# First-branch scores by halves of the rows, and queries split a tile at a time

## What is computed

```python
h = rmsnorm(x, g_mix); z = h @ w_in            # queries, keys, values of both branches, two gates
qa, ka, va, qb, kb, vb, ga, gb = split(z)
# branch A: 8 query heads over 2 key/value heads of 64, per-head rmsnorm, 2-D rotary
q = axial(rmsnorm(qa, q_gain)); k = axial(rmsnorm(ka, k_gain))
s = einsum("bqkgd,bskd->bkgqs", q, k) * scale; o = softmax(s) @ v
# branch B: dilated windows, 3 groups of 4 heads, combined by softmax denominators
x = x + (sigmoid(ga) * (o @ w_a_out) + sigmoid(gb) * (b @ w_b_out)) @ w_out
x = x + square(relu(rmsnorm(x, g_mlp) @ w_up)) @ w_down
```

## Time and profile before

| | us |
|---|---|
| median of 3 runs (1193.88 to 1195.73) | 1195.72 |
| the profiled execution | 1193.6 |
| its span | 1191.8 |
| TensorE busy | 1153.5 (97%) |
| DVE, ACT, POOL busy | 561.5, 414.8, 320.7 |
| share of TensorE in the chain that ended last | 87% |
| first key unit begins / last key unit ends | 40.4 / 87.0 |
| a key unit (81.4 to 87.0) | 5.6 |
| wait for the broadcast of the norms, once, before 56.9 | 3.5 |
| first and last scores of branch A begin | 92.7 / 248.2 |
| waits ahead of scores of branch A at 92.7, 99.9 and 112.0 | 2.0, 1.4, 0.2 |
| product with the values, a prompt unit of A (103.5 to 104.3) | 0.8 |
| granted TensorE clock, mean | 0.994 |

### The profile page before, as it was taken

One profiled execution on the slowest core, in us unless ns is written; L12 is line 12 of the kernel. 1 busy time (PEld: TensorE's weight loads), 2 busy tenths in 40 slices (PEclk: granted clock), 3 DMA queues, 4 the chain that ended last, 5 costly groups with the idle time before them and its releaser, 6 DMA issues.

```text
span 1191.8 us, 16489 instructions
## 1 busy us (share of the span) xinstructions
PE 1153.5 (97%) x6186; PEld 1040.9 (87%) x6186; DVE 561.5 (47%) x1007; ACT 414.8 (35%) x929; POOL 320.7 (27%) x244
## 2 busy tenths in 40 slices
PE   8898999989999999999999999999999999999997
PEld 6776898977889999999788989898898989898896
DVE  7576654555554342422615635344352625344354
ACT  7436666655455321221324312213130212212122
POOL 6311102020111150441713232415041332415120
PEclk9999999999999999999999999999999999999999
DMA  9301020200202030221522012222221112222202
GB/s 349 100 11 61 1 72 1 71 1 3 70 1 72 12 101 19 71 89 57 191 71 69 11 63 71 72 70 70 70 70 37 47 57 70 70 70 70 70 0 106
DMA packets 47125, 77.15 MB, mean 65 GB/s; under 512 B 7648, under 2 KB 18272, under 8 KB 47072
## 3 DMA queue, kind: packets, MB, share of 16 engines
q1 hardware_dynamic: 43488, 71.83, 18.2%
q10 hardware_dynamic: 3584, 4.61, 1.1%
HBM read 73.20 MB, written 3.22 MB: 64 GB/s over the span
## 4 chain that ended last, share of the span: by engine, by line
PE 87%; DVE 7%; issue 3%; ACT 2%; DMA 0%; ACTq 0%; DVEq 0%
PE unit_ps L691 18%; PE unit_ps L692 17%; PE unit_ps L693 17%; PE score_ps L691 7%; PE score_ps L692 7%; PE score_ps L693 7%; PE out_ps L824 4%; PE turn_ps L805 2%; DVE q_lo L1495 1%; PE score_ps L795 1%; PE unit_ps L752 1%; PE score_ps L752 1%; PE out_ps L752 1%; PE score_ps L770 1%; PE turn_ps L919 1%
## 5 line engine op out<-in xcount | busy, mean ns | idle before, releaser
L666 POOL TENSOR_TENSOR ring_lo<-ring_whole,ring_hi 128x512 fp32r<-128x512 f32 x236 | 311.9, 1343 | 832.9 <-ACT ring_hi L951 832.6
L691 PE MATMUL score_ps<-act_hi,ring_hi 128*128 128x384 f32 x512 | 171.3, 335 | 0.0
L693 PE MATMUL score_ps<-act_hi,ring_lo 128*128 128x384 f32 x512 | 171.1, 334 | 0.0
L692 PE MATMUL score_ps<-act_lo,ring_hi 128*128 128x384 f32 x512 | 171.1, 334 | 0.0
L961 ACT ACTIVATE relu<-score_ps 128x384 f32<-128x384 f32 x64 | 31.5, 493 | 380.2 <-PE score_ps L693 380.2
L951 ACT ACTIVATE ring_hi<-ring_whole 128x512 fp32r<-128x512 f32 x236 | 143.5, 625 | 42.0 <-DMA ring_whole<-in_w_up 22.5
L693 PE MATMUL unit_ps<-ring_hi,u_lo 128*128 128x512 f32 x384 | 151.3, 394 | 0.0
L691 PE MATMUL unit_ps<-ring_hi,u_hi 128*128 128x512 f32 x384 | 151.3, 394 | 0.0
L692 PE MATMUL unit_ps<-ring_lo,u_hi 128*128 128x512 f32 x384 | 151.3, 394 | 0.0
L1332 DVE TENSOR_TENSOR x<-x,unit_ps 128x512 f32<-128x512 f32 x96 | 65.8, 686 | 177.2 <-PE unit_ps L693 177.2
L691 PE MATMUL unit_ps<-ring_hi,act_hi 128*128 128x512 f32 x336 | 144.4, 430 | 1.3 <-DVE mix_part L1471 1.2
(11 more groups left out here) (174 smaller groups left out, 1797.2 us busy)
## 6 DMA issues: line engine op xcount, KB each, us to landing
ring_whole<-in_w_up SPq DMA_DIRECT2D x64, 256.0 KB, 4.6
ring_whole<-in_w_down SPq DMA_DIRECT2D x64, 256.0 KB, 4.4
ring_whole<-in_w_in SPq DMA_DIRECT2D x47, 256.0 KB, 4.7
ring_whole<-in_w_in SPq DMA_DIRECT2D x64, 128.0 KB, 2.9
ring_whole<-in_w_out SPq DMA_DIRECT2D x16, 256.0 KB, 4.1
xT<-in_x_turned SPq DMA_DIRECT2D x16, 192.0 KB, 4.7
x_in<-in_x_prompt SPq DMA_DIRECT2D x4, 512.0 KB, 6.8
ring_whole<-in_w_a_out SPq DMA_DIRECT2D x8, 256.0 KB, 4.7
```

Source lines behind the costliest of these rows:

```text
L666: pool.tensor_tensor(ring_lo[:, slot, :], ring_whole[:, slot, :], ring_hi[:, slot, :].bitcast(F32), ALU.subtract).then_inc(lo_cut, 1)
L691: pe.matmul(out, sta[0], mov[0], start=first, stop=False)
L692: pe.matmul(out, sta[0], mov[1], start=False, stop=False)
L693: return pe.matmul(out, sta[1], mov[0], start=False, stop=last)
```

## The change

Scores of branch A are issued for two units at a time, as branch B's are: one of each key head, the one on rows 0 to 63 and the other on rows 64 to 127, three products over 64 rows each. The pair waits for the exponential of the unit before it. The units are ordered so that heads g and g + 4 are neighbours. Queries are rotated by DVE straight from the banks to `q_tok` (the second ACT copy goes; DVE's cosine product frees the bank); the step `turn_q` transposes a whole query tile when its first attention unit is added to the list, and splits it into `q_hi` and `q_lo`, each once, for four heads on both halves of the rows. Keys have one high and one low tile. `scale_q` stands behind the last `take_qa`. At most one tile waits for its transpose in the key units, and there are three token buffers for five.

```diff
-TOK_BUFS = 5
+TOK_BUFS = 3
...
-        branch_a += [("A", t, [(h, 0, 4)]) for h in range(A_HEADS)]
+        branch_a += [("A", t, [(x * A_GROUP + g, 0, 4)]) for g in range(A_GROUP) for x in range(A_KV)]
...
-        branch_a += [("A", t, [(h, 4, 2), (h + 1, 4, 2)]) for h in range(0, A_HEADS, 2)]
+        branch_a += [("A", t, [(h, 4, 2), (h + 1, 4, 2)]) for h in (0, A_GROUP, 2, A_GROUP + 2)]
...
             units.append(new)
-            steps.append(("q_split", len(units) - 1))
+            if new[2][0][0] == 0:
+                steps.append(("turn_q", new[1]))
...
-            paired = i < len(units) and units[i][0] != "A" and i % 2 == 0
-            if paired and units[i - 1][0] != "A":
+            paired = i < len(units) and i % 2 == 0
+            early = paired and i and units[i - 1][0] != "A"
+            if early:
...
     def take_qa(t):
         steps.append(("take_qa", t))
-        waiting.append(("qa", t))
...
             take_qa(t + 2)
-        while len(waiting) > 3:
+            if t + 2 == TILES - 1:
+                steps.append(("scale_q",))
+        while len(waiting) > 1:
             turn_next()
...
-        q_hi = sb(ctx, "q_hi", [P, 2, 2, P], F32R)
-        q_lo = sb(ctx, "q_lo", [P, 2, 2, P], F32R)
+        q_hi = sb(ctx, "q_hi", [P, 2, A_GROUP, P], F32R)
+        q_lo = sb(ctx, "q_lo", [P, 2, A_GROUP, P], F32R)
...
             def scores_a(u):
+
                 _, t, segs = units[u]
-                bank = score_ps[u % 2]
                 if u == 0:
                     pe.wait_ge(qa_free, TILES)
-                pe.wait_ge(queries_split, u + 1)
...
+                else:
+                    pe.wait_ge(expd, u)
+                pe.wait_ge(*free_of(turn_free, plan.turn_no[("turn_q", t)]))
+                for tt in {seg[1] + seg[2] - 1 for seg in segs}:
+                    pe.wait_ge(*free_of(turn_free, plan.turn_no[("turn_qk", "kva", tt)]))
+                for j in range(len(segs)):
+                    for product in range(3):
+                        for x in range(2):
+                            h, k0, nk = units[u + x][2][j]
+                            rows = slice(x * HD, (x + 1) * HD)
+                            q = (q_lo if product == 2 else q_hi)[rows, t % 2, h % A_GROUP, :]
+                            k = (k_lo if product == 1 else k_hi)[rows, k0 * P:(k0 + nk) * P]
+                            last = pe.matmul(score_ps[x][:, j * nk * P:(j + 1) * nk * P], q, k, start=(product == 0),
+                                             stop=(product == 2))
...
+                elif kind == "turn_q":
+                    n, t = plan.turn_no[s], s[1]
+                    pe.wait_ge(q_ready, t + 1)
+                    wait_bank(pe, turn_free, n)
+                    for c in range(A_GROUP):
+                        last = pe.transpose(turn_ps[n % 2][:, c * P:(c + 1) * P], q_tok[:, t, c * P:(c + 1) * P],
+                                            ident[:, :])
+                    last.then_inc(turned, 1)
...
-                act.activation(qk_sq[:, :], bank[:, :], ACT.Square)
-
-                act.activation(buf.rearrange("p (g k d) -> p g k d", g=A_GROUP, k=A_KV),
-                               bank[:, :].rearrange("p (k g d) -> p g k d", k=A_KV, g=A_GROUP),
-                               ACT.Copy).then_inc(qa_free, 1)
+
+                act.wait_ge(qk_squares, plan.square_no[("take_qa", t)])
+                act.activation(qk_sq[:, :], qa_banks[t][:, :], ACT.Square).then_inc(qa_squared, 1)
...
+                elif kind == "scale_q":
+                    act.wait_ge(q_sums, 1)
+                    act.activation(q_scale[:, :], q_scale[:, :], ACT.Sqrt).then_inc(q_roots, 1)
...
+                elif kind == "turn_q":
+                    n, t = plan.turn_no[s], s[1]
+                    act.wait_ge(turned, n + 1)
+                    if t >= 2:
+
+                        act.wait_ge(scored, last_of_tile[t - 2] + 1)
+                    act.activation(q_hi[:, t % 2, :, :], turn_ps[n % 2][:, :].rearrange("p (h t) -> p h t", h=A_GROUP),
+                                   ACT.Copy).then_inc(turn_hi, 1)
...
+            def rotate_q(t):
+
+                bank, buf = qa_banks[t], q_tok[:, t, :]
...
+                dve.wait_ge(qa_squared, t + 1)
+                dve.tensor_reduce(q_scale[:, t * A_HEADS:(t + 1) * A_HEADS],
+                                  qk_sq[:, :].rearrange("p (h d) -> p h d", d=HD), AX_X, ALU.add).then_inc(qk_squares, 1)
...
+                for x in range(2):
+                    dve.tensor_tensor(turned_pairs[:, :, :, x, :], pairs[:, :, :, 1 - x, :],
+                                      sines[:, :, x, :].unsqueeze(1).broadcast_to([P, A_HEADS, 2, 16]), ALU.mult)
...
+                dve.tensor_tensor(buf, bank[:, :].rearrange("p (k g d) -> p k g d", **heads),
+                                  rope_qc[:, pos, :].unsqueeze(1).unsqueeze(1).broadcast_to([P, A_KV, A_GROUP, HD]),
+                                  ALU.mult).then_inc(qa_free, 1)
+                dve.wait_ge(qa_free, t + 1)
+                dve.tensor_tensor(buf, buf, rot_q[:, :].rearrange("p (k g d) -> p k g d", **heads),
+                                  ALU.add).then_inc(q_ready, 1)
...
-                dve.wait_ge(scored, u + 1 if branch == "A" else (u // 2 + 1) * 2)
+                dve.wait_ge(scored, (u // 2 + 1) * 2)
...
+                elif kind == "turn_q":
+                    n, t = plan.turn_no[s], s[1]
+                    dve.wait_ge(turn_hi, plan.split_no[s] + 1)
+                    lo_of_turn(q_hi[:, t % 2, :, :], q_lo[:, t % 2, :, :],
+                               turn_ps[n % 2][:, :].rearrange("p (h t) -> p h t", h=A_GROUP))\
+                        .then_inc(turn_free[n % 2], 1)
```

More of the change, by code:

```diff
@@ L191, in attend @@
                 steps.append(("turn_p", i - 2))
-            if paired and units[i - 1][0] == "A":
+            if paired and not early:
                 steps.append(("scores_pair", i))
@@ L518, in build @@
         keys_hi = sem("keys_hi")
[L519 to L520 removed]
+        qa_squared = sem("qa_squared")
+        q_ready = sem("q_ready")
         scored = sem("scored")
@@ L572, in block_end @@
             return plan.unit_no[("unit", name, 7 if name[0] in "gy" else TILES - 1)] + 1
[L574 to L579, removed]
+        last_of_tile = {units[u][1]: u for u in range(len(units)) if units[u][0] == "A"}
         def class_order(branch, t):
@@ L758, in scores_a @@
                 _, t, segs = units[u]
-                bank = score_ps[u % 2]
                 if u == 0:
                     pe.wait_ge(qa_free, TILES)
-                pe.wait_ge(queries_split, u + 1)
[L763 to L772, removed]
+                else:
[12 more added lines that the diff above has]
+                                             stop=(product == 2))
+                            if product == 2 and j == len(segs) - 1:
+                                last.then_inc(scored, 1)
             def scores_pair(u):
@@ L892, in _ @@
                     last.then_inc(turned, 1)
-                elif kind == "scores" and units[s[1]][0] == "A":
-                    scores_a(s[1])
                 elif kind == "scores_pair":
-                    scores_pair(s[1])
+                    (scores_a if units[s[1]][0] == "A" else scores_pair)(s[1])
                 elif kind == "turn_p":
@@ L1079, in _ @@
                         dst = qkT_c[:, class_buffer(name[2], t), :]
[L1080 to L1081 removed]
                     elif name == "kva":
[L1083 to L1087 removed]
+                        act.activation(k_hi[:, t * P:(t + 1) * P], turn_ps[n % 2][:, 0:P], ACT.Copy).then_inc(keys_hi, 1)
                         continue
@@ L1096, in _ @@
                     take_unit(s[1], s[2])
-                elif kind == "q_split":
-                    u = s[1]
-                    _, t, segs = units[u]
-                    act.wait_ge(*free_of(turn_free, plan.turn_no[("turn_qk", "qa", t)]))
-                    if u >= 2:
-                        act.wait_ge(scored, u - 1)
-                    for out in range(2):
-                        last = act.activation(q_hi[out * HD:(out + 1) * HD, u % 2, 0:len(segs), :], queries(u)[0],
-                                              ACT.Copy)
-                    last.then_inc(queries_hi, 1)
+                elif kind == "turn_q":
[5 more added lines that the diff above has]
+                                   ACT.Copy).then_inc(turn_hi, 1)
                 elif kind == "scores":
@@ L1419, in _ @@
                 elif kind == "take_qa":
-                    rotate_a("qa", s[1])
+                    rotate_q(s[1])
+                elif kind == "scale_q":
+                    scale_queries()
                 elif kind == "norm2":
@@ L1484, in _ @@
                     dve.wait_ge(keys_hi, t + 1)
-                    for kv in range(A_KV):
-                        rows, other = slice(kv * HD, (kv + 1) * HD), slice((1 - kv) * HD, (2 - kv) * HD)
```

(13 more changed lines are left out.)

70 lines of the change are left out of this document (33 added, 37 removed).

## The result

The changed kernel takes 1197.03 us (median of 20 runs, 1196.14 to 1198.35), the kernel before, measured beside it, 1195.46 (20 runs, 1191.55 to 1196.85). The ratio is 1.0017, with an interval of [1.001, 1.0023]: slower, by 1.2 to 2.7 us. The direction was forecast, the size (+10) was not.

A forecast was written before the change was run, and what follows sets the result against it. TensorE, busy in 97% of the span, was taken as the bound. The terms 1.6 - 2.2 + 8.0 + 1.5 + 1.1 + 0 gave +10.0 us on 1193.6, so 1203.6 us; 8-in-10 range 1190 to 1213.

The forecast's parts named there:

- The end: Last two pairs, held by the transposes of the third group's last unit, which do not move: 0 us.
- The other ticks: Remaining branch A ticks: 4.2 us of low-half waits go, 5.3 us of new waits for exponentials come: +1.1 us.
- the early start: First pairs issued inside the last key unit: pair 0 waits 3.8 us, pair 2 5.1, plus clock dips; net +8.0 us.
- PE work of the scores: TensorE's work on branch A's 20 pairs: the saved product in four is eaten by mode switches, 0 us.
- Start of the key units: First key unit starts later because DVE, not ACT's copy, now frees the query bank: +1.6 us.
- Key units 2 to 4: Key tile low-half wait and its clock dip go, -4.0 us; key tile 3's transpose waits 1.8: net -2.2 us.
- Tick 7: Transposes of query tile 1 and key tile 5 take both turn banks; the next wait 3.0 us: +1.5 us.
- the rival in which the halves don't overlap: Branch A pairs: products on the two row halves run in series, giving 1217.6 us; chance 0.08.
- The relief: Rival: DVE is far enough ahead that no new wait replaces the old ones, giving 1181.8 us; chance 0.22.
- the even exchange: Rival: new waits only match those replaced, with the early start at 3.4 us, giving 1195.6 us; chance 0.18.

The follow-up runs named there:

- the cuts moved: POOL's cuts of weight chunks moved off the unit's end in four unit groups: changed kernel 1189.76 us (ratio 0.9957), kernel before 1187.83 us (0.9943).
- the late start: The changed kernel with branch A's first tick three ticks later, where the kernel before had it: 1194.77 us, ratio 1.0006 to the kernel before.
- early maxima: The changed kernel with both maxima of a branch A pair taken at once and unit 1's exponential ahead of the last key unit's root: 1188.58 us, ratio 0.9954.
- free banks: The changed kernel with query tiles 0 and 1 in two transpose banks, so the first key unit needs no wait for DVE: 1194.65 us, ratio 1.0001.
- pair behind the values: The changed kernel with a pair of branch A issued behind its tick's product with the values instead of ahead: 1194.41 us, ratio 1.0001.

## Why the prediction was wrong

The step that failed is "The end: 0": the last two pairs do stand where they stood, 14.9 us behind the first unit of the gates in both kernels (381.61 and 385.21), but the pairs of branch B ahead of them cost 4.0 us less than before. "The other ticks: +1.1" failed next, by 2.9. The waits of the early start, the largest term, were right in kind and near in size.

| step | forecast | found in the rows |
|---|---|---|
| PE work of the scores | 0 | +0.3 |
| Start of the key units | +1.6 | +1.5 |
| Key units 2 to 4 | -2.2 | -3.1 |
| The early start | +8.0 | +6.9 |
| Tick 7 | +1.5 | +2.8 |
| The other ticks | +1.1 | -1.8 |
| The end | 0 | -4.0 |
| sum | +10.0 | +2.6 |

**PE work: right in sum, and by luck.** An odd tick and the even one behind it, with the first product of the unit that follows each, in the changed kernel:

```profile
169.62 0.60 PE L813 MATMUL turn_ps<-ident,probs 128*128 128x128 f32 x4
170.06 1.06 PE L832 MATMUL out_ps<-v_a,probsT 128*128 128x128 f32 x8
170.87 0.60 PE L694 MATMUL unit_ps<-ring_hi,act_hi 128*128 128x512 f32 x1
...
172.48 0.60 PE L813 MATMUL turn_ps<-ident,probs 128*128 128x128 f32 x4
173.01 0.50 PE L777 MATMUL score_ps<-k_hi,q_hi 64*128 64x512 f32 x2
...
173.91 1.16 PE L832 MATMUL out_ps<-v_a,probsT 128*128 128x128 f32 x8
174.82 0.60 PE L694 MATMUL unit_ps<-ring_hi,act_hi 128*128 128x512 f32 x1
```

The pair takes 0.90 us (0.85 forecast) and 0.53 pass ahead of it; the transposes of an odd tick take 0.44. Without the values that is 1.87 us, as forecast, and the rival in which the halves don't overlap is out. But the values behind a pair, which the prediction left out, take 0.91 us (173.91 to 174.82) against 0.81 in the odd tick. With them two ticks take 2.34 + 1.25 = 3.59 us, and before 2 x 1.71 = 3.42 (102.55 to 104.26): 0.17 more a pair, some 3.4 us over the 20 pairs. What hides it was not forecast either. In the kernel before, transposes ahead of a score that is held up took longer than the 0.36 counted:

```profile
170.63 0.60 PE L805 MATMUL turn_ps<-ident,probs 128*128 128x128 f32 x4
171.37 0.50 PE L770 MATMUL score_ps<-kT_a,q_hi 128*128 128x512 f32 x1
```

At nine ticks these transposes took 0.60 to 0.74 us beside any listed wait, some 2.6 us more than counted in all, and nearly all of that is gone. In sum: from the first key unit to the gates' first unit are 326.3 us before (40.41 to 366.68) and 327.4 after (42.89 to 370.28); without the waits inside (21.5 and 20.6) and the dips (5.1 and 6.8) 299.7 and 300.0 are left, +0.3.

**Start, key units, early start, tick 7: right in kind.** Each forecast wait stands in the list. The sizes: key tile 3's transpose waits 1.2 for 1.8 us, against the 2.5 that went, the norms' broadcast is 0.1 shorter, and between 36 and 80 us one dip is left of two; pair 0 waits 2.66 for 3.8, pair 2 4.29 for 5.1, with dips of 1.7 each for 2.5 in all, less the 3.4 of before; tick 7 waits 2.6 for 3.0 (1.5 before), and behind it stands a dip of 1.7 that I had not counted and that two of the other runs, with the same wait, do not have. Taken together these four are +8.1 against +8.9.

**The other ticks: wrong by 2.9.** Waits of 1.6 us at ticks 13 and 19 and of 0.7 at three others were forecast. The changed kernel has 1.33 and 1.06, at one place each. Its timeline at ticks 13, 19 and 31:

```profile
145.67 2.62 POOL L669 TENSOR_TENSOR ring_lo<-ring_whole,ring_hi 128x512 fp32r<-128x512 f32 x2 [9.49 <-ACT ring_hi L967]
145.89 1.27 DVE L1329 TENSOR_TENSOR tok<-tok,rot 128x128 f32<-128x128 f32 x1
...
149.27 0.50 PE L777 MATMUL score_ps<-k_hi,q_hi 64*128 64x512 f32 x2 [1.33 <-ACT probs L1117]
...
170.88 0.29 DVE L1329 TENSOR_TENSOR tok<-tok,rot 128x128 f32<-128x128 f32 x1
...
219.90 0.69 DVE L1232 TENSOR_TENSOR q_lo<-turn_ps,q_hi 128x512 fp32r<-128x512 f32 x1 [4.06 <-ACT q_hi L1104]
```

I took the rotation's length, with its last add of 1.26 us, from one unit for all of them. The add takes that long only beside a pair of cuts, and not every unit has one; at tick 19 it takes 0.29 and the next pair (173.01) waits for nothing. (The three terms written for this chain, 3.1, 0.92 and 0.9, make 4.9 us and not 5.2; with that the wait at tick 13 would have come out at 1.3, as measured.) Of the three waits of 0.7, those behind ticks 25 and 37 did not come, and the 1.06 at 222.42 has a cause I had not named there: on DVE the maximum stands behind the low half of a whole query tile, which falls in the tick behind this unit. The kernel before already had both kinds, 12 long and 4 short (12 x 1.26 + 4 x 0.29 = 16.3, the busy time of its row), and the group's mean of 1017 ns hid them.

**The end: wrong by 4.0, the largest miss.** "The end: 0" followed the last two pairs alone and held branch B for unaffected. But its ticks come three ticks sooner against the unit ends. A unit has three ticks and a pair comes every second one, so a shift by three changes which units have a pair right behind their rotation. Timeline of the kernel before, at the first unit of `qk2`:

```profile
310.07 2.61 POOL L666 TENSOR_TENSOR ring_lo<-ring_whole,ring_hi 128x512 fp32r<-128x512 f32 x2 [32.41 <-ACT ring_hi L951]
...
310.29 1.27 DVE L1313 TENSOR_TENSOR tok<-tok,rot 128x128 f32<-128x128 f32 x1
...
313.14 0.83 PE L795 MATMUL score_ps<-qkT 64*128 64x256 f32 x4 [1.77 <-DVE neg_max L1368]
```

and of the changed kernel at the same unit:

```profile
319.86 1.16 PE L803 MATMUL score_ps<-qkT_c 64*128 64x128 f32 x16
...
320.82 2.63 POOL L669 TENSOR_TENSOR ring_lo<-ring_whole,ring_hi 128x512 fp32r<-128x512 f32 x2 [30.26 <-ACT ring_hi L967]
...
321.03 1.25 DVE L1329 TENSOR_TENSOR tok<-tok,rot 128x128 f32<-128x128 f32 x1
...
326.20 1.13 PE L803 MATMUL score_ps<-qkT 64*128 64x256 f32 x8
```

The cut and the long add are there in both. Before, the pair comes in the tick behind the unit's end and waits for a maximum that stands behind the rotation on DVE; in the changed kernel one pair is issued at the unit's end, ahead of the rotation, and the next two ticks on, when the maxima are done. The waits now fall at the units between. There are four such places in both kernels: before, all four wait (266.90, 288.79, 313.14, 338.21); after, three do (268.57, 290.74, 335.00) and the fourth (312.39) does not, where the add has no cut beside it (310.70, 0.29) and the scores behind it are 256 wide. The place before without a cut (286.92) had scores 512 wide and waited 1.04. So the waits of the banded pairs go from 6.3 to 4.0. Putting the ticks back brought all 6.3 back, so this part is shown. Most of it does not hang on the cuts: with the cuts moved in both kernels the waits are 3.4 and 1.6. The other 1.7 us of the term is the dip of the kernel before at 313 us, which the late start did not have behind the same wait of 1.77 (clock 1.00 from 300 to 350 us), so it is no fixed part of the return.

**The rivals.** The relief did not win, and the even exchange has the nearest number (1195.6) for another reason than it gave: it held the early start for cheap, and that cost 6.9 us. What made the sum small was a return further on, most of it in a branch that the diff does not touch.

## What to carry to other kernels

An edit that moves a step in a shared schedule moves every later step against its neighbours: list which steps then coincide, to the end of the schedule, before a later stage is put at zero. A duration taken from one row of a group with a wide spread needs its condition (what ran beside it), which the extremes of the group tell and its mean does not. Where an engine works a queue in order, look first whether a small result that others wait for stands behind unrelated work: moving the maxima ahead was worth nearly four times what the change itself moved (7.5 us against 2.0).

## What the runs showed of the hardware

- A 128x128 add on DVE with both inputs in SBUF took 1.27 us beside POOL's cut and 0.29 without; a maximum over scores in PSUM that ran beside the same cuts (147.09) took 0.68, as elsewhere. Moving the cuts, ACT's part with POOL's, was worth 6.8 us to the kernel before and 7.2 to the changed one. The Trainium skill, "SBUF — State Buffer", section Who interferes with whom, says that a DVE instruction with two SBUF inputs and a GpSimd instruction that reads SBUF exclude each other, and that the later one waits until the other is finished. The rows agree: the add begins inside the first of two cuts of 1.31 us each and ends at 147.16, 0.2 us after that cut's end.
- The load of the root's table had 0.02 us of idle time at either side: a copy ended at 91.68, the load ran from 91.70 to 92.98, the root began at 93.00. The drain of 1380 ns that the prediction cites from the Trainium skill, "ScalarE: Activation LUTs", section What ACT_TABLE_LOAD costs, is not in this trace; pair 2 waited less than forecast.
- The granted clock fell to 0.57 to 0.59 for some 4 us (0.72 over 6 us at the fourth place), near the lower of its two levels, behind four waits of the changed kernel: 3.41 (the norms' broadcast), 2.66, 4.29 and 2.57 us. In the ten profiles, from 36 to 400 us, the shortest wait with such a dip behind it is 1.77 us and the longest without one 2.58. The same wait can go either way: that of 2.57 or 2.58 at tick 7 was followed by a dip in two runs (the changed kernel, early maxima) and by none in two others (free banks, pair behind the values), and the one of 1.77 in branch B by a dip in the kernel before and by none in the late start. What decides stays open. A wait in this kernel costs its length and, often but not always, 1.7 us more, so a difference of 1.7 us between two profiles need not be the edit's.
